# One inference step of a two-layer hybrid decoder: retention heads in another order, and a layer norm that centres early

## What is computed

```python
Layer l even: x <- LN(ALPHA*x + W_out_ab [ChunkGMLP | StickBreak])
Layer l odd : x <- LN(ALPHA*x + W_out_ret (silu(g) * HeadNorm(Retention(q, k, v))))
Every layer : x <- LN(ALPHA*x + W_down(gelu(causal_dwconv3(x W_gate)) * x W_val))

def _layer_norm(x, g, b):
    mu = jnp.mean(xf, axis=-1, keepdims=True)
    var = jnp.mean(jnp.square(xf - mu), axis=-1, keepdims=True)
    return (xf - mu) * lax.rsqrt(var + LN_EPS) * g + b

def step(S, inp):                       # retention, chunk by chunk, per head
    sc = jnp.einsum('blhd,bmhd->bhlm', qc, kc) * dmat[None]
    o = jnp.einsum('bhlm,bmhe->blhe', sc, vc) + jnp.einsum('blhd,bhde->blhe', qc, S) * q_dec
    S = S * c_dec + jnp.einsum('bmhd,bmhe->bhde', kc * k_dec, vc)
```

## Time and profile before

| what | value |
| --- | --- |
| runs before | 1887.91, 9645.24, 1884.31 us; median 1887.91 |
| the profiled execution's own time | 1884.67 us |
| its span, first to last instruction | 1882.9 us |
| TensorE matmul, busy share | 93% |
| VectorE / ScalarE / GpSimd | 47% / 28% / 8% |
| mean granted TensorE clock | 0.967 of full speed |
| DMA | 234.65 MB, mean 125 GB/s |

### The profile page before, as it was taken

One profiled execution on the slowest core, in us unless ns is written; L12 is line 12 of the kernel. 1 busy time (PEld: TensorE's weight loads), 2 busy tenths in 40 slices (PEclk: granted clock), 3 DMA queues, 4 the chain that ended last, 5 costly groups with the idle time before them and its releaser, 6 DMA issues.

```text
span 1882.9 us, 35054 instructions
## 1 busy us (share of the span) xinstructions
PE 1756.8 (93%) x13474; PEld 1589.9 (84%) x13474; DVE 890.6 (47%) x1435; ACT 528.2 (28%) x742; POOL 151.3 (8%) x137
## 2 busy tenths in 40 slices
PE   8998996979999999979989989989987999999996
PEld 8766674869999999969679769859947999999995
DVE  3444455556552455352372273264256655245544
ACT  3324333232221222132222222222223322122213
POOL 0000002001000000004013013013010100000000
PEclk9999999989999999999989989989988999999998
DMA  8888784112232222212342332333422222222221
GB/s 287 295 294 285 258 303 173 45 45 86 82 109 71 88 89 92 87 46 89 119 146 96 129 128 101 141 117 106 152 100 78 83 88 96 84 78 89 98 85 48
DMA packets 84222, 234.65 MB, mean 125 GB/s; under 512 B 9778, under 2 KB 10067, under 8 KB 83779
## 3 DMA queue, kind: packets, MB, share of 16 engines
q1 hardware_dynamic: 80834, 218.97, 33.9%
q0 software_dynamic: 3328, 14.92, 2.2%
HBM read 210.05 MB, written 23.80 MB: 124 GB/s over the span
## 4 chain that ended last, share of the span: by engine, by line
PE 66%; issue 24%; DVE 6%; ACT 2%; POOL 1%; DMA 1%; SPq 0%; DVEq 0%; POOLq 0%; ACTq 0%
PE banks L1267 50%; PE banks L1612 2%; PE banks L1532 2%; PE banks L1604 2%; PE banks L1294 1%; PE banks L1369 1%; PE banks L1592 1%; PE banks L1382 1%; PE banks L1621 1%; PE banks L1330 1%; POOL y L417 1%; PE banks L1358 1%; PE banks L1372 1%; DVE x_lo L1034 1%; DVE s L1144 1%
## 5 line engine op out<-in xcount | busy, mean ns | idle before, releaser
L1267 PE MATMUL banks<-x_hi,w_hi 128*128 128x272 f32 x2624 | 551.7, 292 | 33.0 <-DVE x_lo L1034 21.9
L1267 PE MATMUL banks<-x_hi,w_lo 128*128 128x272 f32 x2624 | 545.6, 290 | 0.0
L1267 PE MATMUL banks<-x_lo,w_hi 128*128 128x272 f32 x2624 | 544.8, 289 | 0.0
L694 DVE TENSOR_TENSOR w_lo<-w_raw,w_hi 128x1024 fp32r<-128x1024 f32 (+2 forms) x228 | 282.7, 1240 | 519.6 <-ACT w_hi L462 519.4
L462 ACT ACTIVATE w_hi<-w_raw 128x1024 fp32r<-128x1024 f32 (+2 forms) x228 | 238.2, 1045 | 941.6 <-PE banks L1267 911.2
L1267 PEld LDWEIGHTS banks<-x_hi,w_hi 128*128 128x128 f32 x2624 | 415.3, 190 | 51.1 <-issue 33.3
L1267 PEld LDWEIGHTS banks<-x_lo,w_hi 128*128 128x128 f32 x2624 | 416.1, 190 | 0.0
L1267 PEld LDWEIGHTS banks<-x_hi,w_lo 128*128 128x128 f32 x2624 | 413.4, 190 | 0.0
L1267 PE MATMUL banks<-act_lo,w_hi 128*128 128x272 f32 x704 | 145.2, 287 | 0.0
L1267 PE MATMUL banks<-act_hi,w_hi 128*128 128x272 f32 x704 | 145.0, 287 | 0.0
L1267 PE MATMUL banks<-act_hi,w_lo 128*128 128x272 f32 x704 | 145.0, 287 | 0.0
(11 more groups left out here) (232 smaller groups left out, 1704.6 us busy)
## 6 DMA issues: line engine op xcount, KB each, us to landing
w_raw<-in_w_up SPq DMA_DIRECT2D x88, 512.0 KB, 3.2
kv<-in_kc SPq DMA_DIRECT2D x128, 256.0 KB, 4.5
kv<-in_vc SPq DMA_DIRECT2D x128, 256.0 KB, 4.3
w_raw<-in_w_rin SPq DMA_DIRECT2D x48, 512.0 KB, 3.2
w_raw<-in_w_dn SPq DMA_DIRECT2D x32, 704.0 KB, 4.0
s<-in_s SPq DMA_DIRECT2D x32, 512.0 KB, 8.7
out_ret_s<-s SPq DMA_DIRECT2D x32, 512.0 KB, 2.6
w_raw<-in_w_in_ab POOLq DMA_DIRECT2D x16, 512.0 KB, 5.1
```

The source lines that it names most:

```text
L694: V.tensor_tensor(w_lo[:, j, 0:k * P], w_raw[:, j, 0:k * P], w_hi[:, j, 0:k * P].bitcast(F32), ALU.subtract).then_inc(lo_ready, 1)
L1267: last = mm(B[:, 2 * j + half, 0:HN], a[:, j, w], x[:, kt, half * HN:(half + 1) * HN], start=kt == 0 and n == 0, stop=kt == k - 1 and n == 2)
```

## The change

The loop over heads is written out in code on every engine, and inside a head the order is another:

- The transposes of keys and values stand in pairs between the last input tiles, on TensorE, ScalarE and VectorE alike.
- The samples' outputs come before the prompt's, the samples' head norm first. The prompt's state is computed last, in two pieces around the transposes of the last output block.
- The samples' state updates leave the middle: one stands behind each output tile. In the last head it is two, and three state steps stand ahead of the tiles.
- SyncE loads states and weights alternately, and stores a state after each output tile; the next head's first four weight tiles are loaded among them.

The norm is built into the product ahead of it (`summed_product`). After three tiles (four in the last head) the mean of the first two blocks is taken and subtracted from all blocks, from those to come before their product is added. Squares are summed pair by pair, in four strips of 32 rows, during the last tiles. After the product the difference of this provisional mean to the true one is taken, its square is subtracted from the variance, and VectorE shifts and scales the blocks. ScalarE now adds the norm's shift into `y` itself and then makes the hi part. The first tile behind norms 0 to 2 is computed by plain fp32 matmuls from `w_raw` and `y` (`first_pair`), the second waits for hi and lo parts as before. GpSimd's scaling of the residual comes after that first tile.

The diff, cut to its core:

```diff
+FIRST = [U_FFN[0], U_RET, U_FFN[1]]
...
+PLAIN = [3, 3, 4, 3]
+BACK = (0, 1, 2, 7)
...
+                if isinstance(u, int) and u - 2 in FIRST:
+                    sp.wait_ge(tile_done, u - 1)
...
-            with sp.Fori(0, H_C) as h:
+            for h in range(H_C):
...
+                def load_out(i):
                     load(A["w_rout"], h * N_OUT + i, base + (N_RIN + i), i % 2, 4)
+                for i in range(0 if h == 0 else 4, N_RIN):
+                    load(A["w_rin"], h * N_RIN + i, base + i, i % 2, KD)
...
+                    if i >= 4:
+                        load_state(i - 4)
+                for i in range(4):
+                    load_out(i)
+                store_state(0)
+                for i in range(N_OUT):
+                    if i < 4:
+                        load_out(i + 4)
+                    elif h < H_C - 1:
+                        load(A["w_rin"], (h + 1) * N_RIN + i - 4, base + N_RET + i - 4, i % 2, KD)
+                    elif i < 6:
+                        load(A["w_up"], 2 * N_UP + i - 4, U_FFN[1] + i - 4, i % 2, KD)
+                    store_state(i + 1)
...
-            with pool.Fori(0, H_C) as h, step.loop(h, H_C, 8):
+            for h in range(H_C):
...
+                take_output(NB, 3)
+                deviation(0, NB, NB + 1)
+                for t in range(NB - 1):
+                    take_output(t, t)
+                deviation(1, 0, NB - 1)
+                take_output(NB - 1, 6)
+                deviation(2, NB - 1, NB)
+                affine(0)
+                affine(1)
+                high(0)
+                affine(2)
+                high(1)
+                affine(3)
+                high(2)
+                high(3)
...
+                nc.scalar.activation(halves(std[:, :]), B[:, 4:6, 0:HN], ACT.Square).then_inc(shift_sq, 1)
...
+                def centre(m):
+                    dve.wait_ge(first_mean, n + 1)
+                    if m < plain:
+                        dve.wait_ge(evicted[m % 2], (base + m) // 2 + 2)
+                    V.scalar_tensor_tensor(halves(y[:, m, :]), B[:, 4:6, 0:HN], -4.0, halves(y[:, m, :]), ALU.mult,
+                                           ALU.add).then_inc(c_ready if m < plain else c_early, 1)
...
+                dve.wait_ge(var_done, n + 1)
+                dve.wait_ge(shift_sq, n + 1)
+                V.tensor_tensor(halves(s1[:, :]), B[:, 6:8, 0:HN], halves(std[:, :]), ALU.subtract).then_inc(var_ready, 1)
+                for m in range(3):
+                    shift(m)
                 dve.wait_ge(std_ready, n + 1)
...
+                for m in range(3):
+                    scale(m)
+                for m in range(3, KD):
+                    shift(m)
+                    scale(m)
+                if n < 3:
+                    low(FIRST[n] + 1, 1, KD)
+                    for m in range(KD):
                         dve.wait_ge(lnhi_ready, n * KD + m + 1)
-                        V.scalar_tensor_tensor(x_lo[:, m, :], y[:, m, :], lnp[:, n, 1, m:m + 1],
-                                               x_hi[:, m, :].bitcast(F32), ALU.add, ALU.subtract)\
+                        V.tensor_tensor(x_lo[:, m, :], y[:, m, :], x_hi[:, m, :].bitcast(F32), ALU.subtract)\
...
+                inverse(0, NB, NB + 1)
+                normed(NB, NB + 1)
+                stats(0, NB - 1)
+                variance(0, NB - 1)
+                inverse(1, 0, NB - 1)
+                normed(0, NB - 1)
+                gate_samples()
+                stats(NB - 1, NB)
+                variance(NB - 1, NB)
+                inverse(2, NB - 1, NB)
+                normed(NB - 1, NB)
+                gate(0)
+                gate(1)
+                gate_low(0)
+                gate(2)
                 gate_low(1)
-                inverse(1, NB, NB + 1)
-                normed(NB, NB + 1)
+                gate(3)
                 gate_low(2)
                 gate_low(3)
-                gate_samples()
...
+                state(0)
+                if h == H_C - 1:
...
+                    dve.wait_ge(y_scaled, 1 + 2 * KD)
+                    for i in range(N_OUT):
+                        dve.wait_ge(tile_done, base + (N_RIN + i + 1))
+                        V.tensor_tensor(halves(y[:, i, :]), halves(y[:, i, :]), bank_pair(i % 2), ALU.add)\
+                            .then_inc(evicted[i % 2], 1)
+                        low(base + (N_RIN + i + 2), i % 2, 4 if i < N_OUT - 2 else KD)
+                        state(i + 1)
...
+            def partial_mean(n):
+                pe.wait_ge(first_sum, n + 1)
                 for half in range(2):
-                    last = mm(B[:, 4 + half, 0:HN], mean_mat, s1[:, half * HN:(half + 1) * HN], start=True, stop=True)
-                last.then_inc(m_done, 1)
-                for m in range(KD):
-                    pe.wait_ge(sq_ready, n * KD + m + 1)
+                    last = mm(B[:, 4 + half, 0:HN], mean_mat, s1[:, cols(half)], start=True, stop=True)
+                last.then_inc(first_mean, 1)
+            def partial_squares(n, pair):
+                pe.wait_ge(sq_ready, n * KD + 2 * pair + 2)
+                for g in range(4):
+                    half, row = g // 2, g % 2
+                    last = mm(B[32 * g:32 * g + 32, 6 + half, 0:HN], mean_mat[:, 0:32], sq[:, row, cols(half)],
+                              start=pair == 0, stop=pair == 2)
+                last.then_inc(sq_used, 1)
+            def square_sums(n):
+                pe.wait_ge(part_ready, 2 * n + 2)
+                for half in range(2):
+                    part = slice(64 * half, 64 * half + 64)
+                    mm(B[:, 6 + half, 0:HN], ones[part, :], std[part, 0:HN], start=True, stop=False)
+            def row_6(n):
+                pe.wait_ge(rest_sum, n + 1)
+                pe.wait_ge(c_ready, sum(PLAIN[:n + 1]))
+                pe.wait_ge(c_early, sum(KD - p for p in PLAIN[:n + 1]))
+                for half in range(2):
+                    mm(B[:, 4 + half, 0:HN], mean_mat, s1[:, cols(half)], start=True, stop=False)
+                square_sums(n)
+                pe.wait_ge(sq_ready, n * KD + 7)
+                for half in range(2):
+                    mm(B[:, 6 + half, 0:HN], mean_mat, sq[:, 0, cols(half)], start=False, stop=False)
+            def row_7(n, base):
+                pe.wait_ge(evicted[1], base // 2 + 5)
+                for half in range(2):
+                    last = mm(B[:, 4 + half, 0:HN], mean_mat, y[:, 7, cols(half)], start=False, stop=True)
+                last.then_inc(shift_done, 1)
+                pe.wait_ge(sq_ready, n * KD + 8)
+                for half in range(2):
+                    last = mm(B[:, 6 + half, 0:HN], mean_mat, sq[:, 1, cols(half)], start=False, stop=True)
+                last.then_inc(var_done, 1)
+            def summed_product(n, base, k, hi, lo, k_ready=None, behind=None):
+                for i in range(N_OUT):
+                    pe.wait_ge(lo_ready, base + i + 1)
+                    pe.wait_ge(evicted[i % 2], (base + i) // 2 + 1)
+                    if i < 7:
+                        tile_body(i % 2, k, hi, lo, k_ready if i == 0 else None)
+                    else:
+                        part_body(1, k, hi, lo, range(k // 2))
+                        partial_squares(n, 1 if k == 4 else 2)
+                        part_body(1, k, hi, lo, range(k // 2, k - 1))
+                        if k > 4:
+                            row_6(n)
+                        part_body(1, k, hi, lo, range(k - 1, k))
+                    if behind:
+                        behind(i)
+                    if i == PLAIN[n] - 1:
+                        partial_mean(n)
+                    if k > 4 and i == 5:
+                        partial_squares(n, 0)
+                    if i == 6:
+                        partial_squares(n, 0 if k == 4 else 1)
+                if k == 4:
+                    partial_squares(n, 2)
+                    row_6(n)
+                row_7(n, base)
+            def first_pair(n):
+                u = FIRST[n]
+                pe.wait_ge(lo_ready, u + 1)
+                pe.wait_ge(evicted[0], u // 2 + 1)
+                for kt in range(KD):
+                    pe.wait_ge(whole_ready, n * KD + kt + 1)
                     for half in range(2):
-                        last = mm(B[:, 6 + half, 0:HN], mean_mat, sq[:, m % 2, half * HN:(half + 1) * HN],
-                                  start=m == 0, stop=m == KD - 1)
-                    last.then_inc(sq_used, 1)
+                        last = mm(B[:, half, 0:HN], w_raw[:, 0, kt * P:(kt + 1) * P], y[:, kt, cols(half)],
+                                  start=kt == 0, stop=kt == KD - 1)
+                last.then_inc(tile_done, 1)
+                pe.wait_ge(lo_ready, u + 2)
+                pe.wait_ge(evicted[1], u // 2 + 1)
+                tile_body(1, KD, x_hi, x_lo, lambda kt: pe.wait_ge(ln_done, n * KD + kt + 1))
...
+                pe.wait_ge(roped, h * 4 + 4)
```

(62 more changed lines are left out.)

459 lines of the change are left out of this document (254 added, 205 removed).

## The result

The changed kernel takes 1814.0 us (median of four, 1812.7 to 1814.2) against 1886.1 of the kernel before: a ratio of 0.962, 95% interval 0.960 to 0.964. Its profiled execution took 1812.68 us, 72.0 less than that of before. One run of the kernel before, of 9645.24 us, is a slow one and does not enter the ratio. The forecast was 1812, range 1798 to 1840.

The account below looks back on a forecast made before the run. TensorE, busy 93% of the span, was taken as the bound, so only its waits and lower clock could give. From 1884.7 us: -43.8 + 3.0 - 19.1 - 10.8 + 0 - 1.9 = -72.6, giving 1812, range 1798 to 1840.

Parts of the forecast that it names:

- The heads: Four heads: the middle becomes dense, period 133.9 us against 148.5; terms -43.8, +3.0 and -19.1.
- The state matmuls: Sample state updates in a head: 8 x 2 matmuls of 512 columns, taken at 4.0 us between 3.8 and 7.0.
- The 0.5 for the sample scores: Middle of each head: 0.5 us added to the period for the sample scores on VectorE.
- VectorE in an output tile: Output tiles: VectorE needs 2.63 us, 3.15 beside GpSimd, under TensorE's 3.5, so it is fast enough.
- The norms: Norms 0 and 1: 5.2 inside the product plus 26.3 behind it, 31.5 us against 36.9, -5.4 each.
- The product's extra work: Product ahead of a norm: partial mean, square sums and six more matmuls on TensorE, 5.2 us, 9.1 if serial.
- under the vector chain: Norms 0 and 1: first fp32 tile ends by 19.4 us; VectorE's chain to the third weight tile, 26.3, ends last.
- Norm 3: Last norm, up to the end of the span: 26.2 us against 28.1, -1.9.
- Norm 2: Head 3's output tiles and the norm behind them: 63.1 us against 62.8, called 0, give or take 3.
- B: Output tiles: the state wait comes back, 1.0 us a tile over 32 tiles, 1844 us; chance 0.19.
- C: Written-out heads: instruction packets stop TensorE, 35 more at 2.7 us each, 95 us, 1907; chance 0.04.
- D: Whole kernel better than forecast, under 1799 us, with square sums and states nearly free; chance 0.03.

Follow-up runs that it names:

- Experiments 1 to 3: Changed kernel, each undoing one move: state updates in one block (heads 0 to 2), 1844.0 us; prompt state ahead of prompt outputs, 1843.3; transposes behind last input tile, 1817.9.
- Experiment 4: Changed kernel with the first tile behind norms 0 to 2 in three passes of high and low parts instead of fp32: 1835.4 us.
- experiment 7: Changed kernel with head 3's eight state updates moved behind tiles 2 to 9 of the second ConvFFN: 1809.3 us, repeated 1809.5 against 1817.6.
- experiment 6: Kernel before the change with only its loop over the four heads written out on all five engines: 1885.4 us, ratio 0.9992.
- experiment 3: Changed kernel with the four key and value transposes behind the last input tile again: 1817.9 us.
- experiment 2: Changed kernel with the prompt state done ahead of the prompt outputs again: 1843.3 us.
- experiment 8: Kernel with head 3's updates in the second ConvFFN, plus GpSimd taking the mean shift of the last four tiles of y in all norms: 1814.2 us.

## Why the prediction was right

**The sum.** The heads came out 3.2 us better than forecast (-63.1 against -59.9), the four norms 3.5 worse (rows 1, 2, 5 and 6 of the table). That the profiled execution came within 1 us of the forecast is luck: the two cancel. The range's ends were no sums: the terms named for the upper end come to more than 1840 if all are added.

**The heads.** The period was put at 133.9 and is 133.3. The wait of the state chain, the norm handoffs and the lower clock were taken as gone, and all three are. Experiments 1 to 3 show that no move did it alone: 27 to 30 us hang on the updates' place in three heads, 28 to 29 on the prompt state's in four, 3 to 4 on the transposes'. That is about the 63 us that the heads gained, though costs of single moves undone need not add up. The samples' outputs ahead of the prompt's and SyncE's new order were not undone; what they bring is open. The state matmuls were taken at 4.0 a head between 3.8 and 7.0; they are 8 x 0.47 = 3.8. The 524 ns a matmul of the earlier trace rows are a mean over two clocks: in head 1 of the kernel before a pair took 0.71 to 0.74 us at clock 1.00 and 1.22 at 0.50. The 0.5 for the sample scores is the 0.53 in the chain.

**VectorE in an output tile.** The low part was expected drawn out by GpSimd, by less than a whole GpSimd operation, and no wait came of it; in the six tiles beside the masking (0.92 us of GpSimd) it takes 0.92 to 0.93 us instead of 0.69, and the state update behind it stays at 1.27.

**The norms.** Norm 0 was right to 0.5 us, norm 1 to 1.3, the parts less so. The product's extra work was put at 5.2 and is 6.0 in norm 0 (55.8 from the product's start to its end, against 49.8) and some 6.4 in norm 1: a group of square sums takes 0.6, not 0.5, and each change between the kinds of matmul costs a little more (24 matmuls between two groups take 3.20 us instead of 3.0). Behind the product, 26.3 was forecast and 26.0 and 26.2 measured from the last take, but what ends last was named wrong. The first fp32 tile does not end at 19.4 "under the vector chain": it ends at 20.0, on the lower clock for its first 6 us, and the second tile follows it. The first of these stretches (columns as in the earlier trace rows):

```profile
409.00:412.00 3.00, 3.00 (x7) 2.31 (x8) 2.93 (x5) 2.30 (x4) 0.00 (x0) 0.50 0.00 0
```

In norms 0 and 1 the third tile then waits for its weights as well: the load cannot start until the fp32 tile has left the raw weights, and lands 3.5 us later (the split at 423.11). That wait, which the prediction had not listed, costs 0.1 and 0.6 us, and VectorE stands still for 1.28 us of norm 0, where the prediction had it unbroken up to the third tile's weights.

Part of norm 1's gain has another cause. In the kernel before, VectorE waited there for GpSimd, which scaled the residual and then zeroed a buffer (`qm`), and TensorE waited for VectorE's low part (VectorE's timeline, then TensorE's):

```profile
849.68 0.07 DVE L1097 MEMSET rmv<- 128x10 f32 x1 [7.11 <-POOL qm L426]
...
851.37 0.49 PE L1267 MATMUL banks<-x_hi,w_hi 128*128 128x272 f32 x2 [1.73 <-DVE w_lo L694]
```

The changed kernel asks for both only later, inside the heads. So in norm 1 of before two tiles were done 35.1 us behind the take, not the 36.9 of norm 0 that the prediction used for both, and 1.7 more were this wait. That the two come to nearly the same 36.9 is chance; of norm 1's 4.1 us, 1.7 are a wait that the prediction had not seen.

The two halves of the norm's change do not pay alike. Experiment 4 leaves early centring in and takes the fp32 tile out: norms 0 and 1 are then 2 to 3 us slower than before the change. Norm 3, which has no tile behind it, gained 0.9. So the gain of norms 0 and 1, but for the 1.7 us above, hangs on the fp32 tile; what that tile would bring without early centring was not tried and stays open.

**Norm 2 and norm 3.** 0 give or take 3 came out as +0.7; experiment 7 shows the cost inside it, two updates on a tile. Norm 3's -1.9 was -0.9: the product's extra is 6.6 us instead of 5.2, and from the last take to the end it takes 20.6.

**The rivals.** B, the waits in the output tiles, is out by the chain above: none in heads 0 to 2. C, instruction loading, is out by experiment 6 and by the chain of a head, in which TensorE waits for no packet. The Trainium skill, "Runtime: NRT & Kernel Launch", section "Instruction fetch mechanics", holds that straight code is fetched ahead; the 0.9992 agrees. The stall at a far branch, from which the prediction had written-out heads save something, does not show in it. D was near on the heads (3.76 for the states) but not on the norms.

## What to carry to other kernels

A chain that goes back and forth between two engines is worth splitting into single steps and laying each behind a piece of work longer than the step: here 1.27 us behind 3.0 us of matmuls, and one update to a tile cost TensorE its own 0.47 us, while two made it wait. Price the piece to be moved at the rate of its new place, not at its old mean, which may hold a lower clock. Where a chain cannot be split, look for independent work of the same engine to stand in its place, as the prompt state does, and check that each cover is worth its own gain by undoing one at a time.

## What was not expected of the hardware

A VectorE operation on two SBUF operands can be drawn out far more beside GpSimd than the row of 1.79 in the earlier trace rows said. In experiment 3's profile, in the input tiles of head 0, a low part that takes 1.23 us elsewhere, in VectorE's timeline:

```profile
858.00 5.25 DVE L762 TENSOR_TENSOR w_lo<-w_raw,w_hi 128x1024 fp32r<-128x1024 f32 x1 [4.79 <-ACT w_hi L481]
```

And GpSimd's timeline beside it:

```profile
858.16 6.29 POOL L455 TENSOR_TENSOR onat<-rqk,rope 128x544 f32<-128x544 f32 x4
```

It took 5.25 us beside GpSimd's rotation; one in experiment 2's profile took 5.25 as well, and in the changed kernel's profile the second low part took 2.40. The Trainium skill, "SBUF — State Buffer", section "Who interferes with whom", holds that such an operation contends with a GpSimd operation that reads SBUF, and that the lock between them is exclusive; the prediction weighed this at 3.6 us an output tile and set it aside. The runs lie between that rule and the row. In the output tiles the low part grew by 0.23 us, less than the 0.52 of the row. Here VectorE stood nearly as long as the rule would have it, yet it ended at 863.25, before GpSimd's fourth operation did (864.45). In experiment 8 the first of the two steps ended at 410.24, while GpSimd worked until 411.42 (a profile gives GpSimd's spans only roughly). So the price beside GpSimd has to be measured at the place in question.
